# Row loads on ScalarE's queue, chunk loads first on SyncE's, GpSimd's broadcasts held back, and the first operands split by pairs

## The chip, the cores and the metric

One core of a Trainium2 chip runs the whole program. The metric is the device time of one execution in microseconds, as the median of several runs. Beside the timed runs there is one profiled execution, from which every row below is taken.

## The reference, cut to what matters

Two transformer stages run one after the other on 256 tokens of width 1024, in fp32. What matters here is how the first one begins:

```
mod   = silu(c)     @ w_ada + b_ada          # c: 1024 numbers, w_ada: 1024 x 6144
mod_c = silu(c_ctx) @ w_ada + b_ada
h  = rmsnorm(x,   g_norm1) * (1 + sc1)  + sh1
hc = rmsnorm(ctx, g_norm1) * (1 + scc1) + shc1
p, p_c = h @ w_in, hc @ w_in                 # 1024 x 2592
```

Everything after (attention, retention, the three feed-forward parts, the second stage's mixers) depends on `p` and `p_c`.

## The kernel before

**Precision by splitting.** TensorE multiplies in a fast format, so each fp32 matrix is split in two: ScalarE copies it into a rounded high part (`wh`, `hh`, `ch`), VectorE subtracts that from the original to get the low part (`wl`, `hl`, `cl`), and `three` issues three matmuls for a product (lines 1920 to 1922).

**Modulation.** The first 2048 columns of `w_ada` come as eight chunks of 128 rows, 1 MB each, `mod1_w[0]` to `mod1_w[7]`. TensorE takes them in the order 0, 1, 3, 2, 4, 5, 6, 7. Chunks 1, 2, 4, 5 and 7 are split (`mod1_high`, line 1485, on ScalarE, then `mod1_low`, line 803, on VectorE); 0, 3 and 6 are used as they are. After chunk 3 TensorE turns the small vectors, which lie as rows of `vrow`, into columns, and VectorE needs these before it normalises `ctx` and splits chunk 4. After chunk 2 TensorE turns the normalised `ctx`. After chunk 7 the sums are turned, `mod` is formed, and `mod1_ready` lets the operands be made.

**Small vectors.** `VEC_TILES` lists 16 row loads in three tiles: three with `c`, `c_ctx` and `c_2` first (`FIRST_ROWS`), eight more in tile 0, four in tile 1, one in tile 2. `in_c` counts the first three, `in_rows` the others, `in_ident` the identity matrix, a part of `con`. Before the chunks, TensorE turns the first three and ScalarE takes their silu; `cs_ready` then lets TensorE begin chunk 0.

**Queues.** SyncE issues nearly all loads, in an order written by hand: the three rows, the identity, chunks 0 to 2, the 13 remaining rows, chunk 3, `ctx`, chunks 4 and 5, `x`, chunks 6 and 7, then the units of `w_in` (each up to 1 MB, in two parts). GpSimd issues at its start four small broadcasts (`in_small`), clears `acc` and loads its bias, and loads `postg`, a 512 KB broadcast that is wanted much later. Behind these in GpSimd's program comes a wait for work of about 74 us. ScalarE issues no loads.

**The first operands.** `evac_high` (line 1462) on ScalarE and `evac_low` (line 744) on VectorE make `ch`/`cl` (N_CTX) and then `hh`/`hl` (N_X) in four pairs j of two row blocks each. For a pair, ScalarE forms block 2j in `hraw[:, 0]` and VectorE block 2j+1 in `hraw[:, 1]`, both from PSUM; then ScalarE copies both to the high part, one at a time, and VectorE subtracts, one at a time. ScalarE's second copy alone waits for VectorE's block. VectorE splits unit 1 (`take(1)`) between pairs 1 and 2 of `ctx`. TensorE starts the products of either operand when two pairs of `hraw` have been read out of PSUM (`t_raw`, `d_raw`).

Of the kernel before, what the change touches and what calls it, by code (L numbers as in the profile page):

```python
# [7 lines left out]
ALU = mybir.AluOpType  # L8
ACT = mybir.ActivationFunctionType
AX = mybir.AxisListType  # L10
F32 = mybir.dt.float32
# [4 lines left out]
P = 128  # L16
TOK = 256
# [34 lines left out]
def shape_constants():  # L52
# [19 lines left out]
    for name, f in (("cos_m", np.cos), ("sin_m", np.sin)):  # L72
# [7 lines left out]
VEC_TILES = [  # L80
# [3 lines left out]
    [("conv_w", 88 * P, 44)],  # L84
]
# [32 lines left out]
N_CTX, N_X, N_RET, N_FF0, N_MIX1, N_FF1, N_KV, N_MIX2, N_FOX, N_FF2 = range(10)  # L118
# [80 lines left out]
FIRST_ROWS = 3  # L199
# [5 lines left out]
def build(nc, a, out):  # L205

    ctx = ExitStack()
    with ctx:
# [7 lines left out]
        con = sb("con", [P, CONST_W])  # L216
# [12 lines left out]
        hraw = sb("hraw", [P, 2, HALF])  # L229
# [23 lines left out]
        vrow = junk[:, 0:3 * P].rearrange("p (t c) -> p t c", t=3)  # L253
# [127 lines left out]
        in_c = sem("in_c")  # L381
        in_ident = sem("in_ident")
# [7 lines left out]
        d_raw = sem("d_raw")  # L390
        in_rows = sem("in_rows")
# [7 lines left out]
        mod1_loaded = [sem(f"mod1_loaded{i}") for i in range(6)]  # L399
# [31 lines left out]
        t_hi = sem("t_hi")  # L431
        t_lo = sem("t_lo")
# [145 lines left out]

        taken = []

        block = ctx.enter_context(nc.Block())


        @block.vector
        def _(dve):
# [158 lines left out]
            def evac_low(n, lo, hi, pairs):  # L744

                for j in pairs:
                    k = 2 * j + 1
                    dve.wait_ge(turned, 4 * TURN_NO[n] + 2 * (j // 2) + 2)
                    dve.wait_ge(t_lo, 8 * n + max(k - 3, 0))
                    at = (j % 2) * TOK  # L750
                    nc.vector.tensor_scalar(hraw[:, 1, at:at + TOK], ps[:, TURN_BANKS[n][2 * (j // 2) + 1], at:at + TOK],  # L751
                                            mod[:, n, 0, k:k + 1], mod[:, n, 1, k:k + 1], ALU.mult, ALU.add)\
                        .then_inc(d_raw, 1)
                    for side in range(2):
                        kk = 2 * j + side
                        dve.wait_ge(t_hi, 8 * n + kk + 1)
                        nc.vector.tensor_tensor(lo[:, kk, :], hraw[:, side, at:at + TOK], hi[:, kk, :].bitcast(F32),
                                                ALU.subtract).then_inc(t_lo, 1)
# [461 lines left out]
            for t in range(NT):  # L1220
                c = R_AT[R_KH] + t * FH
# [48 lines left out]
            for t in range(NT):  # L1270
                c = R_AT[R_QH] + t * FH
# [40 lines left out]
            for h in range(FH):  # L1312
# [7 lines left out]
                else:  # L1320
                    v = FOX_ADA + h // 8
# [31 lines left out]
        def _(act):  # L1353
# [103 lines left out]
            def root_table():  # L1457

                nc.scalar.activation(credit[:, used[0]:used[0] + 1], ident[:, 0:1], ACT.Sqrt)
                used[0] += 1  # L1460

            def evac_high(n, hi, pairs):

                for j in pairs:
                    k = 2 * j
                    act.wait_ge(turned, 4 * TURN_NO[n] + 2 * (j // 2) + 1)
                    act.wait_ge(t_lo, 8 * n + max(k - 3, 0))
                    at = (j % 2) * TOK
                    nc.scalar.activation(hraw[:, 0, at:at + TOK], ps[:, TURN_BANKS[n][2 * (j // 2)], at:at + TOK],  # L1469
                                         ACT.Identity, scale=mod[:, n, 0, k:k + 1], bias=mod[:, n, 1, k:k + 1])\  # L1470
                        .then_inc(t_raw, 1)
                    act.wait_ge(t_raw, 4 * n + j + 1)
                    nc.scalar.activation(hi[:, k, :], hraw[:, 0, at:at + TOK], ACT.Copy).then_inc(t_hi, 1)
                    act.wait_ge(d_raw, 4 * n + j + 1)
                    nc.scalar.activation(hi[:, k + 1, :], hraw[:, 1, at:at + TOK], ACT.Copy).then_inc(t_hi, 1)

            def mod1_high(i, parts=(slice(0, UNIT),)):
# [6 lines left out]
                for cc in parts:  # L1484
                    nc.scalar.activation(wh[:, SPLIT_SLOT[i], cc], mod1_w[k][:, cc], ACT.Copy).then_inc(m_hi, 1)

            act.wait_ge(in_ident, 16)
            nc.scalar.activation(credit[:, 15:16], ident[:, 0:1], ACT.Silu)
            act.wait_ge(c_cols, 1)
# [3 lines left out]
                .then_inc(cs_ready, 1)  # L1493
            act.wait_ge(cs0_zero, 1)
            nc.scalar.activation(cs0[:, 0:2], cs[:, 0:16:8], ACT.Copy).then_inc(cs_ready, 1)
            root_table()
            mod1_high(0)
            mod1_high(1)
# [1108 lines left out]
        def _(pool):  # L2607
# [11 lines left out]
            def start_acc(g):  # L2619

                if g > 1:

                    pool.wait_ge(ex_done, EX_BASE[g])
                nc.gpsimd.memset(acc[:, :], 0.0).then_inc(acc_zeroed, 1)  # L2624
                pool.wait_ge(acc_zeroed, g)
                pool.dma_start(acc[0:1, :], ada[g][1]).then_inc(acc_biased, 16)
# [14 lines left out]
            def load_bc(j):  # L2641
# [5 lines left out]

            nc.gpsimd.memset(credit[:, 0:1], 0.0).then_inc(hid_pool, CREDIT)
            nc.gpsimd.memset(credit[:, 1:2], 0.0).then_inc(gl_done, CREDIT)
            pool.dma_start(lg[:, 3, :], a["ret_decay"][0].rearrange("d h -> (d h)").partition_broadcast(P))\  # L2650
                .then_inc(in_small, 16)
            pool.dma_start(bf[:, :], a["kv_b_f_2"].partition_broadcast(P)).then_inc(in_small, 16)
            pool.dma_start(gcol[0:FD, 0:1], a["b_q_norm_g_2"][0].rearrange("(d c) -> d c", c=1)).then_inc(in_small, 16)
            pool.dma_start(gcol[0:FD, 1:2], a["k_norm_g_2"].rearrange("(d c) -> d c", c=1)).then_inc(in_small, 16)
            start_acc(1)
            load_postg(0)

            pool.wait_ge(sq_done, SQ_NO[R_C, 0, 5] + 1)
# [82 lines left out]
        def _(sp):  # L2741
# [40 lines left out]
                k = v % 8  # L2782
                sp.dma_start(au[:, v % 2, :], ada[v // 8][0][k * P:(k + 1) * P, :]).then_inc(au_loaded[v % 2], 16)

            def send_rows(t, first, last):

                r = sum(n for _, _, n in VEC_TILES[t][:first])
                for name, at, n in VEC_TILES[t][first:last]:
                    v = a[name]
                    if len(v.shape) == 2:  # L2790
                        v = v.rearrange("a b -> (a b)")
                    elif len(v.shape) == 3:
                        v = v.rearrange("a b c -> (a b c)")
                    sp.dma_start(vrow[r:r + n, t, :], v[at:at + n * P].rearrange("(r c) -> r c", c=P))\
                        .then_inc(in_c if name in ("c", "c_ctx", "c_2") else in_rows, 16)
                    r += n

            def send_chunk(k):
                sp.dma_start(mod1_w[k], ada[0][0][k * P:(k + 1) * P, :])\
                    .then_inc(au_loaded[k] if k < 2 else mod1_loaded[k - 2], 16)  # L2800

            send_rows(0, 0, FIRST_ROWS)
            sp.dma_start(con[:, 0:P], a["shape_consts"][:, 0:P]).then_inc(in_ident, 16)
            for k in range(3):
                send_chunk(k)
            send_rows(0, FIRST_ROWS, len(VEC_TILES[0]))
            for t in (1, 2):
                send_rows(t, 0, len(VEC_TILES[t]))
            send_chunk(3)
            sp.dma_start(cx[:, :, :], a["ctx"][0].rearrange("(t p) d -> p t d", p=P)).then_inc(in_ctx, 16)  # L2810
            send_chunk(4)
            send_chunk(5)
# [74 lines left out]
```

## Time and profile before

| | us |
|---|---|
| median of 3 runs | 1173.5 (1172.95 to 1174.92) |
| the profiled execution, its own time | 1174.02 |
| its span from first to last instruction | 1172.2 |
| TensorE busy | 1134.3 (97%) |
| VectorE, ScalarE, GpSimd busy | 832.2, 602.7, 209.8 |

The share of TensorE is nearly full over the whole span except in the first slices, so the stretch up to about 67 us is read instruction by instruction. The 1.8 us between own time and span lie outside the instructions.

### The profile page before, as it was taken

How to read it: one execution, taken by the hardware profiler on the slowest of the kernel's cores; microseconds unless marked ns; L12 is line 12 of the kernel's file. 1: busy time of each engine (PE TensorE's matmuls, PEld its weight loads, DVE VectorE, ACT ScalarE, POOL GpSimd, SP SyncE). 2: the span in 40 equal slices, each digit the busy share in tenths (PEclk: the TensorE clock that was granted, in tenths of full speed). 3: DMA queues.
4: the chain of work that ended last, by engine and by line, in shares of the span. 5: the costliest groups of instructions: out<-in, count | busy, mean ns of one | idle time of the engine just before them, and what ended most of it. 6: DMA issues, size and time to landing. Idle time of an engine off the chain costs nothing.

```text
span 1172.2 us, 18295 instructions
## 1 busy us (share of the span) xinstructions
PE 1134.3 (97%) x7112; PEld 984.5 (84%) x7112; DVE 832.2 (71%) x908; ACT 602.7 (51%) x884; POOL 209.8 (18%) x164
## 2 busy tenths in 40 slices
PE   5899989999999999999999999999999999999998
PEld 1587747889999877798879999887878988999986
DVE  3795565778887967988777765967889797354543
ACT  4863354556665446454365444346456667444433
POOL 1037400005666302010001112100000000122200
PEclk9999999999999999999999999999999999999999
DMA  8685650148876886986547887874888334556551
GB/s 329 261 321 191 233 215 2 36 134 297 280 262 215 324 349 204 339 268 210 206 144 270 299 274 251 324 302 172 321 283 294 123 105 144 180 179 185 195 195 72
DMA packets 124304, 263.38 MB, mean 225 GB/s; under 512 B 8329, under 2 KB 76497, under 8 KB 114001
## 3 DMA queue, kind: packets, MB, share of 16 engines
q1 hardware_dynamic: 121553, 254.56, 61.6%
q0 software_dynamic: 2688, 7.95, 2.3%
q8 instruction: 43, 0.70, 0.2%
q14 instruction: 20, 0.16, 0.0%
HBM read 261.43 MB, written 1.05 MB: 224 GB/s over the span
## 4 chain that ended last, share of the span: by engine, by line
PE 79%; DVE 8%; ACT 4%; DMA 4%; issue 3%; SPq 1%; DVEq 0%; ACTq 0%
PE ps L1920 23%; PE ps L1922 23%; PE ps L1921 23%; DVE wl L599 2%; DMA raw<-in_w_in_dram 2%; PE ps L2226 1%; ACT wh L1361 1%; PE ps L2242 1%; PE ps L1961 1%; DVE vg L1155 1%; DMA raw<-in_kv_w_dram 1%; DMA raw<-in_w_down_dram 1%; PE ps L2277 1%; PE ps L2285 1%; PE ps L2234 1%
## 5 line engine op out<-in xcount | busy, mean ns | idle before, releaser
L599 DVE TENSOR_TENSOR wl<-raw,wh 128x2048 fp32r<-128x2048 f32 (+2 forms) x149 | 342.9, 2304 | 106.6 <-ACT wh L1361 105.7
L1361 ACT ACTIVATE wh<-raw 128x2048 fp32r<-128x2048 f32 (+2 forms) x148 | 278.8, 1890 | 138.2 <-DMA raw<-in_ffn_w_down_dram 52.9
L1920 PE MATMUL ps<-hh,wh 128*128 128x256 f32 (+1 forms) x1192 | 337.9, 283 | 4.7 <-DVE wl L599 3.6
L1921 PE MATMUL ps<-hl,wh 128*128 128x256 f32 (+1 forms) x1192 | 334.9, 281 | 0.0
L1922 PE MATMUL ps<-hh,wl 128*128 128x256 f32 (+1 forms) x1192 | 334.8, 281 | 0.0
L1920 PEld LDWEIGHTS ps<-hh,wh 128*128 128x128 f32 (+1 forms) x1192 | 223.9, 188 | 6.8 <-DVE wl L599 3.6
L1921 PEld LDWEIGHTS ps<-hl,wh 128*128 128x128 f32 (+1 forms) x1192 | 223.9, 188 | 0.3
L1922 PEld LDWEIGHTS ps<-hh,wl 128*128 128x128 f32 (+1 forms) x1192 | 223.8, 188 | 0.2
L1920 PE MATMUL ps<-wh,hh 128*128 128x512 f32 (+1 forms) x352 | 138.8, 394 | 5.6 <-DVE hraw L751 2.5
L611 DVE SCALAR_TENSOR_TENSOR acc<-au,cs,acc 128x2048 f32<-128x2048 f32 x53 | 129.6, 2446 | 13.2 <-DMA acc<-in_ada_b_dram 8.6
L2701 POOL TENSOR_TENSOR gl<-hid,gh 128x256 f32 (+1 forms) x66 | 78.7, 1192 | 324.8 <-ACT gh L1709 324.8
L1921 PE MATMUL ps<-wl,hh 128*128 128x512 f32 (+1 forms) x352 | 136.3, 387 | 0.0
L1922 PE MATMUL ps<-wh,hl 128*128 128x512 f32 (+1 forms) x352 | 136.3, 387 | 0.0
L1920 PE MATMUL ps<-wh,gh 128*128 128x512 f32 x264 | 104.9, 397 | 0.1
L1921 PE MATMUL ps<-wl,gh 128*128 128x512 f32 x264 | 104.3, 395 | 0.0
L1922 PE MATMUL ps<-wh,gl 128*128 128x512 f32 x264 | 104.2, 395 | 0.0
L1920 PEld LDWEIGHTS ps<-wh,hh 128*128 128x128 f32 x352 | 66.7, 190 | 23.1 <-ACT hraw L1469 2.6
L1694 ACT ACTIVATE sl<-ps 128x256 f32<-128x256 f32 x44 | 16.9, 385 | 126.4 <-PE ps L1922 126.4
L1922 PEld LDWEIGHTS ps<-wh,hl 128*128 128x128 f32 x352 | 66.7, 189 | 14.6
L1921 PEld LDWEIGHTS ps<-wl,hh 128*128 128x128 f32 x352 | 66.8, 190 | 13.6 <-issue 0.2
L2624 POOL MEMSET acc<- 128x2048 f32 x9 | 16.3, 1815 | 320.1 <-PE ps L2065 283.1
L1067 DVE TENSOR_TENSOR hid<-sl,ps 128x256 f32<-128x256 f32 x44 | 18.3, 417 | 62.1 <-ACT sl L1694 62.1
(325 smaller groups left out, 1602.1 us busy)
## 6 DMA issues: line engine op xcount, KB each, us to landing
au<-in_ada_w_dram SPq DMA_DIRECT2D x48, 1024.0 KB, 6.1
raw<-in_ffn_w_gu_dram SPq DMA_DIRECT2D x88, 512.0 KB, 4.8
raw<-in_w_up_dram SPq DMA_DIRECT2D x44, 512.0 KB, 4.8
raw<-in_ffn_w_down_dram SPq DMA_DIRECT2D x44, 512.0 KB, 4.5
au<-in_w_ada_dram SPq DMA_DIRECT2D x18, 1024.0 KB, 6.7
raw<-in_a_w_in_dram SPq DMA_DIRECT2D x32, 512.0 KB, 6.2
raw<-in_w_down_dram SPq DMA_DIRECT2D x22, 512.0 KB, 6.4
raw<-in_w_in_dram SPq DMA_DIRECT2D x16, 512.0 KB, 6.6
```

Source lines behind the costliest of these rows:

```text
L599: nc.vector.tensor_tensor(wl[:, u % RAW, 0:n], raw[:, u % RAW, 0:n], wh[:, u % RAW, 0:n].bitcast(F32), ALU.subtract).then_inc(lo_done, 1)
L611: nc.vector.scalar_tensor_tensor(acc[:, :], au[:, v % 2, :], cs[:, at:at + 1], acc[:, :], ALU.mult, ALU.add).then_inc(acc_step, 1)
L1067: nc.vector.tensor_tensor(hid[:, c, :], sl[:, c, :], ps[:, 4 + pp % 4, TOK:], ALU.mult)\
L1155: nc.vector.tensor_tensor(part, part, bcast(bc[:, j % 4, :], 1, NT), op).then_inc(affine, 1)
L1361: nc.scalar.activation(wh[:, u % RAW, 0:n], raw[:, u % RAW, 0:n], ACT.Copy).then_inc(hi_done, 1)
L1694: nc.scalar.activation(sl[:, c, :], ps[:, bank, 0:TOK], ACT.Silu).then_inc(silu_done, 1)
L1920: nc.tensor.matmul(to, lh, rh, start=start, stop=False, skip_group_check=True)
L1921: nc.tensor.matmul(to, lh, rl, start=False, stop=False, skip_group_check=True)
L1922: return nc.tensor.matmul(to, ll, rh, start=False, stop=stop, skip_group_check=True)
L1961: ins = nc.tensor.matmul(ps[:, EX_BANKS[g][0], j:j + 1], acc[:, c * P:(c + 1) * P], ones[:, 0:1], start=True, stop=True, skip_group_check= ...
L2624: nc.gpsimd.memset(acc[:, :], 0.0).then_inc(acc_zeroed, 1)
L2701: nc.gpsimd.tensor_tensor(gl[:, at_, :], hid[:, c:c + 1, :], gh[:, at_, :].bitcast(F32), ALU.subtract)\
```

## The change

Four things move. The row loads and the identity go from SyncE's program to ScalarE's: the first twelve ahead of the silu, the five of tiles 1 and 2 behind it. SyncE begins with chunks 0 to 3 and keeps the rest of its order. GpSimd clears `acc` and loads its bias first, then waits until chunk 7 has landed, and only then issues the four small broadcasts and `postg`. And for all four pairs of N_X and pairs 1 to 3 of N_CTX, ScalarE waits for both blocks and copies them in one instruction of 512 columns, and VectorE subtracts both in one.

```
+        def paired(n, j):
+            return n == N_X or (n == N_CTX and j >= 1)
...
+                    if paired(n, j):
+                        dve.wait_ge(t_hi, 8 * n + 2 * j + 2)
+                        nc.vector.tensor_tensor(lo[:, 2 * j:2 * j + 2, :], hraw[:, :, at:at + TOK],
+                                                hi[:, 2 * j:2 * j + 2, :].bitcast(F32), ALU.subtract).then_inc(t_lo, 2)
+                        continue
...
+                    if paired(n, j):
+                        act.wait_ge(d_raw, 4 * n + j + 1)
+                        nc.scalar.activation(hi[:, k:k + 2, :], hraw[:, :, at:at + TOK], ACT.Copy).then_inc(t_hi, 2)
+                        continue
...
+            send_rows(0, 0, FIRST_ROWS)
+            act.dma_start(con[:, 0:P], a["shape_consts"][:, 0:P]).then_inc(in_ident, 16)
+            send_rows(0, FIRST_ROWS, len(VEC_TILES[0]))
             act.wait_ge(in_ident, 16)
...
+            for t in (1, 2):
+                send_rows(t, 0, len(VEC_TILES[t]))
             root_table()
...
+            start_acc(1)
+            pool.wait_ge(mod1_loaded[5], 16)
             pool.dma_start(lg[:, 3, :], a["ret_decay"][0].rearrange("d h -> (d h)").partition_broadcast(P))\
                 .then_inc(in_small, 16)
...
-            start_acc(1)
             load_postg(0)
...
-            send_rows(0, 0, FIRST_ROWS)
-            sp.dma_start(con[:, 0:P], a["shape_consts"][:, 0:P]).then_inc(in_ident, 16)
-            for k in range(3):
+            for k in range(4):
                 send_chunk(k)
-            send_rows(0, FIRST_ROWS, len(VEC_TILES[0]))
-            for t in (1, 2):
-                send_rows(t, 0, len(VEC_TILES[t]))
-            send_chunk(3)
```

`send_rows` itself is moved from SyncE's program to ScalarE's, with `act.dma_start` in place of `sp.dma_start`.

## Rows read from the trace of the kernel before

**Rows 1.** Busy time from 66 us on: engines PE, PEld, DVE, ACT, POOL, clock.

```profile
66.00:1172.00 1106.00, 1085.22 (x6861) 954.96 (x6859) 793.24 (x846) 564.87 (x825) 204.31 (x151) 1.00 0.63 220
```

**Rows 2.** Stretches: us, PE, PEld, DVE, ACT, POOL busy, granted clock, DMA share, GB/s.

```profile
20.00:34.00 14.00, 12.22 (x53) 4.58 (x52) 9.78 (x15) 9.07 (x14) 0.00 (x0) 1.00 1.02 417
...
49.24:51.68 2.44, 0.00 (x0) 0.03 (x1) 1.86 (x5) 2.22 (x6) 0.00 (x0) 1.00 0.00 0
53.50:56.00 2.50, 2.50 (x13) 2.50 (x13) 1.67 (x4) 2.41 (x4) 0.00 (x0) 0.50 0.00 0
57.00:67.00 10.00, 10.00 (x80) 9.83 (x78) 8.57 (x5) 2.09 (x2) 0.00 (x0) 1.00 0.80 272
```

**Rows 3.** Timeline of ScalarE up to its first split of a chunk.

```profile
4.78 0.20 ACT L1488 ACTIVATE credit<-con 128x1 f32<-128x1 f32 x1 [2.75 <-DMA con<-in_shape_consts_dram]
...
5.69 1.28 ACT L1459 ACT_TABLE_LOAD   x1
...
13.39 1.91 ACT L1485 ACTIVATE wh<-au 128x2048 fp32r<-128x2048 f32 x1 [6.20 <-DMA au<-in_w_ada_dram]
```

**Rows 4.** Timeline of VectorE, the splits of chunks 1, 4 and 5.

```profile
15.33 2.29 DVE L803 TENSOR_TENSOR mod_l<-au,wh 128x2048 fp32r<-128x2048 f32 x1 [9.38 <-ACT wh L1485]
...
26.68 4.67 DVE L803 TENSOR_TENSOR mod_l<-mod_w,wh 128x2048 fp32r<-128x2048 f32 x2 [0.19 <-ACT wh L1485]
```

**Rows 5.** Timeline of TensorE: chunk 0, chunk 1, first product of h.

```profile
10.33 6.14 PE L2092 MATMUL ps<-au,cs 128*4 128x512 f32 x8 [5.23 <-DMA au<-in_w_ada_dram]
17.77 0.39 PE L2081 MATMUL ps<-wh,cs 128*4 128x512 f32 x1 [1.29 <-DVE mod_l L803]
...
51.68 0.35 PE L1920 MATMUL ps<-wh,hh 128*128 128x256 f32 x1 [2.45 <-DVE hraw L751]
```

**Rows 6.** Timeline of VectorE around one pair of h.

```profile
51.05 0.54 DVE L751 TENSOR_SCALAR hraw<-ps,mod 128x256 f32<-128x256 f32 x1
51.57 0.92 DVE L757 TENSOR_TENSOR hl<-hraw,hh 128x256 fp32r<-128x256 f32 x2
52.41 0.54 DVE L751 TENSOR_SCALAR hraw<-ps,mod 128x256 f32<-128x256 f32 x1
```

**Rows 7.** Timeline of SyncE's queue: start us, length us, line and operation.

```profile
0.75 0.40 SPq L2794 DMA_DIRECT2D hraw<-in_c_dram  x1
...
2.28 0.90 SPq L2799 DMA_DIRECT2D au<-in_w_ada_dram  x2
...
3.70 0.84 SPq L2794 DMA_DIRECT2D hraw<-in_g_norm_dram  x1
...
5.38 0.25 SPq L2794 DMA_DIRECT2D hraw<-in_g_ret_dram  x1
...
7.27 0.38 SPq L2794 DMA_DIRECT2D hraw<-in_conv_w_dram  x1
...
9.34 0.35 SPq L2799 DMA_DIRECT2D mod_w<-in_w_ada_dram  x1
...
14.48 18.32 SPq L2764 DMA_DIRECT2D raw<-in_w_in_dram  x8
```

**Rows 8.** Timeline of ScalarE around the same pair.

```profile
51.12 0.42 ACT L1473 ACTIVATE hh<-hraw 128x256 fp32r<-128x256 f32 x1
51.62 0.42 ACT L1475 ACTIVATE hh<-hraw 128x256 fp32r<-128x256 f32 x1
```

**Rows 9.** Instructions on the chunks' tiles: durations ns, minimum, median and maximum.

```profile
L1485 ACT ACTIVATE wh<-mod_w x5: 1042/1905/1916, 16.7 to 35.6; 128x2048 fp32r<-128x2048 f32 x3, 128x1024 fp32r<-128x1024 f32 x2
L803 DVE TENSOR_TENSOR mod_l<-mod_w,wh x5: 1220/2291/2293, 18.7 to 36.9; 128x2048 fp32r<-128x2048 f32 x3, 128x1024 fp32r<-128x1024 f32 x2
```

**Rows 10.** Timeline of ScalarE, a 512-wide instruction.

```profile
74.54 0.80 ACT L1544 ACTIVATE mask<-con,lg 128x512 f32<-128x512 f32 x1
```

**Rows 11.** Timeline of VectorE: the split of unit 5.

```profile
86.08 2.29 DVE L599 TENSOR_TENSOR wl<-raw,wh 128x2048 fp32r<-128x2048 f32 x1
```

**Rows 12.** Timeline of TensorE: the first product of unit 5.

```profile
90.39 0.39 PE L1920 MATMUL ps<-wh,hh 128*128 128x512 f32 x1
```

More of the change, by code:

```diff
@@ L1485, in mod1_high, with send_rows @@
                     nc.scalar.activation(wh[:, SPLIT_SLOT[i], cc], mod1_w[k][:, cc], ACT.Copy).then_inc(m_hi, 1)
+            def send_rows(t, first, last):
+                r = sum(n for _, _, n in VEC_TILES[t][:first])
+                for name, at, n in VEC_TILES[t][first:last]:
+                    v = a[name]
+                    if len(v.shape) == 2:
+                        v = v.rearrange("a b -> (a b)")
+                    elif len(v.shape) == 3:
+                        v = v.rearrange("a b c -> (a b c)")
+                    act.dma_start(vrow[r:r + n, t, :], v[at:at + n * P].rearrange("(r c) -> r c", c=P))\
+                        .then_inc(in_c if name in ("c", "c_ctx", "c_2") else in_rows, 16)
+                    r += n
+            send_rows(0, 0, FIRST_ROWS)
+            act.dma_start(con[:, 0:P], a["shape_consts"][:, 0:P]).then_inc(in_ident, 16)
+            send_rows(0, FIRST_ROWS, len(VEC_TILES[0]))
             act.wait_ge(in_ident, 16)
@@ L2783, in send_ada @@
                 sp.dma_start(au[:, v % 2, :], ada[v // 8][0][k * P:(k + 1) * P, :]).then_inc(au_loaded[v % 2], 16)
[L2785 to L2796, printed above, removed]
             def send_chunk(k):
```

## The prediction

> **What bounds the kernel now.** I read the shares of busy time first. From 66 us to the end TensorE is busy for 1085 of 1106 us, at its full granted clock [rows 1]. Whatever starts that stretch earlier or later therefore moves the end by as much, unless VectorE or ScalarE falls so far behind that TensorE waits. The change touches nothing after it. So I read the first 66 us, engine by engine, in the timelines.
>
> There the loads look like the limit, since they run at 417 GB/s with a full share from 20 to 34 us [rows 2], but the instruction that waits longest says otherwise from chunk 1 on. Chunk 1 lands at 13.39 us, and ScalarE, which had been idle, splits it at once [rows 3]. VectorE follows at 15.33 [rows 4], and TensorE uses it at 17.77 [rows 5]. From landing to use that is 4.38 us. From 17.77 on TensorE has almost no gap: chunk 3, the turned columns, chunk 2, the turned `ctx`, then chunk 4, which waits for VectorE. VectorE in turn had waited just 0.19 us for ScalarE at 26.68 [rows 4]; its time there comes from the turned columns, hence from TensorE. The stretch up to the operands is thus a chain through TensorE and VectorE with the loads close behind. Its start is the use of chunk 1.
>
> Then the operands are made, and TensorE waits 2.45 us for the second pair of `h` before it starts at 51.68 [rows 5]. That product has 12 matmuls to a row block; at 80 in 10 us [rows 2] these take 1.5 us, so 3.0 us to a pair, and VectorE makes a pair in 1.36 us (51.05 to 52.41, [rows 6]). After the start nothing is short; only the start counts.
>
> **The loads.** SyncE issues chunk 0 at 2.28 us and would now do so at 0.75, that is 1.53 us earlier [rows 7]. Chunk 3, now issued at 9.34, goes out before 3 us. `postg` puts 512 KB, at 417 GB/s 1.25 us of transfer, ahead of chunk 7; its issue, now among GpSimd's first, goes behind that chunk. Landings should therefore come 1.5 us earlier at the start and up to 3.5 us earlier at chunk 7. I take chunk 1 at 13.39 − 1.53 = 11.86 us at the latest.
>
> **ScalarE's queue.** Now every issue costs time on ScalarE. No row of before shows an issue there; SyncE's are the nearest. The first four took from 0.75 to 2.28, the next eight from 3.70 to 7.27, the last five from 7.27 to 9.34 [rows 7]: 1.53 + 3.57 + 2.07 = 7.17 us, 0.42 each. So the twelve end at 0.75 + 1.53 + 3.57 = 5.85. The table load of 1.28 us that now hides in the wait for the identity comes after them: 7.13. The silu and its copies take what lies between 4.78 and 5.69 [rows 3], so TensorE may begin chunk 0 at about 8.0. It takes 6.14 us [rows 5], to 14.2 us. The five others end at 10.1, the next table load and its touch (1.49) at 11.6. That is just when chunk 1 lands at the latest, so its split starts at 11.6 to 11.9 and TensorE uses it 4.38 us later, at 16.0 to 16.2 in place of 17.77. Gain 1.8 us. Two small waits go as well, VectorE's 0.19 us for chunk 4 and about as much at the second half of chunk 7: together 0.4. The head gains **2.2 us**. What is late next is again this same chain; the row loads, which `in_rows` waits for at about 22 us, are there by far.
>
> Both sides: at 0.25 us an issue (the shortest, 5.38 in [rows 7]) ScalarE is free at 8.7, chunk 0 can start at 7 and end at 13.1, and chunk 1 is used no earlier than 13.9: gain 3.9 + 0.4 = 4.3. At the other end each issue could cost more than 0.42; at 0.53 the whole gain of chunk 1 is gone, at 0.84 (3.70 in [rows 7]) it turns into a loss of 5 us. Between these I take the mean, because seventeen issues of this very kind gave it.
>
> The Trainium skill, page "DMA: Bandwidth & Descriptors", section "Issuing engines are not separate DMA queues", speaks against moving issues: the same sixteen engines carry them whoever issues, and only the issuing sequencer's time is saved. By that rule alone the head gains at most the 1.53 us of issue time ahead of chunk 0. The trace of before has one hardware queue only and can't decide it.
>
> **GpSimd's order.** The bias of `acc` comes sooner, and is first wanted when `h` is done. The four small broadcasts go out behind chunk 7, at about 31 us; ScalarE waits for them once it has made `h`, over 20 us later. Behind GpSimd's new wait stand these issues, `postg`, and then work that starts at about 74 us. Nothing is late, and the loads left then are units of `w_in`; the DMA engines are idle at 49 us (share 0.00, [rows 2]). Cost nothing; if the small ones took over 20 us, it would show as a wait before `lg`, up to what they are late.
>
> **The pairs.** Here I expect a loss. Now VectorE's step to the next pair is its own work: raw 0.52 (51.05 to 51.57), then two subtractions of 0.42 [rows 6], while ScalarE's copies run beside it: the first, at 51.12, before VectorE's block is ready, the second, at 51.62, beside the first subtraction [rows 8]. In the new form nothing overlaps: VectorE's block, then ScalarE's copy of both, then the subtraction of both. Prices: block to copy 51.62 − 51.05 = 0.57. The 512-wide copy from the slope of the 1024- and 2048-wide ones, (1.905 − 1.042)/1024 = 0.84 ns a column: 0.61, with the handover 0.65. The subtraction likewise, 1.22 − 512 × 1.046 ns = 0.68 [rows 9], of which 0.61 passes before the next may start. Sum 1.83 us for a pair against 1.36.
>
> Through the order of before: pair 0 of `ctx` is unchanged and the products of `ctx` start as now. Pair 1's subtraction delays the split of unit 1 by 0.48. Pairs 2 and 3 add 0.47 and 0.28 (one shares its time with a wait that is already there). Pair 0 of `h` adds 0.3. So the second block of `h` is ready **1.5 us** later, counted from the start of the operands, and the product of `h` with it. Bounds: if a 512-wide instruction took no longer than a 256-wide one (0.42, [rows 8]), a pair would take 0.57 + 0.46 + 0.42 = 1.45 and the delay be 0.3; with 0.80 for either, the longest 512-wide row [rows 10], a pair takes 2.1 and the delay is 2.4. I stay with the slope, which comes from the same copies and subtractions.
>
> Saved instructions elsewhere give nothing back: ScalarE and VectorE reach the later work some 1.2 us late against TensorE. The tightest place I found is the split of unit 5, which ends at 86.08 + 2.29 = 88.4 [rows 11] and is wanted at 90.39 [rows 12]. The 2.0 us of room cover it; without them it would cost the 1.2 us.
>
> **The clock.** In the 2.44 us before 51.68 TensorE does nothing, and from 53.5 to 56 its granted clock is 0.50, the 1.2 GHz level [rows 2]. At half speed for some 3 us it loses 1.5 us. The new kernel has the same idle, about 2.7 us, and a further one of 1 us within the `ctx` product. I expect the same loss again, and take 0 to 3 us in all as possible.
>
> **The sum.** Own time of the profiled execution 1174.0; head −2.2; pairs +1.5; GpSimd 0; clock 0: 1173.3 us. The median of the runs lies 0.5 under the profiled one, so I forecast **1173.0**.
>
> **Rivals.**
> (a) ScalarE's issues are cheap or the row loads free the chunks: head −4.3 us, pairs +1.5, so 1171.2, or 1170.7 as a median. For it: the table load and the issues hide before chunk 1 if they are short. Against: 0.42 us is a mean of seventeen.
> (b) The head gains only the 1.53 us of earlier issue, as the page's rule above would have it. The sum is then 1174.0 − 1.5 + 1.5 = 1174.0, or 1173.5: no change that shows.
> (c) Slower: the issues on ScalarE stall. SyncE's queue is full at 14.48, where eight issues take 18.32 us, 2.29 each [rows 7]. SyncE now fills it by about 5 us. If ScalarE's last five issues then cost 2.29, it is free 9.4 us later, at 21.0, chunk 1 is used at 25.4, and the head loses 7.6: 1174.0 + 7.6 + 1.5 = 1183. It decides once ScalarE is free later than 15.5 us. Against: the units of `w_in` that took 2.29 have many short rows, and row loads between full queues at 7 to 9 us took 0.4.
> (d) The clock is low for a second stretch, or at chunk 3: +1.5 us, 1174.5. Or not at all: 1171.5.
> (e) The pairing does not lengthen the path, because VectorE's wait overlaps something not seen: 1171.5.
>
> **How the numbers follow.** The forecast with its neighbour (b), 1172 to 1174.5: 0.45. Case (a) 0.15, (e) and no low clock 0.15, (d) slower 0.13, (c) in some degree 0.12. Within 0.2% is 2.35 us, about what a measurement can tell here: 1171.15 to 1175.85. Case (a) is faster by that in full, (e) and no low clock in most of their cases, the forecast in some where its terms are all at the good end: faster 0.36. Slower are (c) and a part of (d): 0.17. Same 0.47. The range 1170.0 to 1176.5 leaves out (c) and the far end of (a). The forecast's own range is 1171.5 to 1174.7.
>
> **What would show it.** ScalarE's queue: seventeen issues, the silu after 7 us, free near 11.6. Chunk 1 used at about 16 us; chunk 7 landed near 31 and the operands begun near 39.4, not 41.55. Pairs of `h` at 1.83 us on VectorE, with a wait for ScalarE in each; the product of `h` near 51.0. A pace of 1.4 us there would prove the pair term wrong; a ScalarE busy with issues past 13 us, or chunk 1 used before 15, the head term.

## The result, and the profile after

The changed kernel takes 1177.44 us (1175.38 to 1179.29) against 1173.96 (1172.95 to 1175.84) for the kernel before, 20 runs of each on one chip. The ratio is 1.0026, with a 95% interval of 1.0020 to 1.0032: **3.1 us slower** (the medians lie 3.5 apart; every difference below is taken from the ratio). In the tests below a few executions ran far longer than the rest, up to 2877 us, and count in the medians but not in the ratios. The forecast was 1173.0 and the range ended at 1176.5; the prediction had given slower a chance of 0.17, and for another reason.

The profiled execution took 1178.46 us with a span of 1176.6, 4.4 more than before. I read the rows in the order of the prediction's steps. First ScalarE's timeline (start us, duration, line, operation; in brackets the idle time before it and what ended it):

```profile
0.74 0.60 ACTq L1509 DMA_DIRECT2D hraw<-in_c_dram  x1
...
2.03 0.41 ACTq L1514 DMA_DIRECT2D con<-in_shape_consts_dram  x1
...
5.77 1.28 ACT L1517 ACT_TABLE_LOAD   x1 [5.77 <-issue]
9.96 0.20 ACT L1517 ACTIVATE credit<-con 128x1 f32<-128x1 f32 x1 [2.92 <-DMA con<-in_shape_consts_dram]
...
12.41 1.28 ACT L1468 ACT_TABLE_LOAD   x1 [1.55 <-issue]
...
13.81 1.89 ACT L1498 ACTIVATE wh<-au 128x2048 fp32r<-128x2048 f32 x1
...
40.90 0.56 ACT L1478 ACTIVATE hraw<-ps,mod 128x256 f32<-128x256 f32 x1
```

The issues are as priced: twelve between 0.74 and 5.74 us, 0.42 each, and five from 10.55 to 12.37, 0.36 each. But the silu, which was to run as soon as they and the table load were over (7.05), waits 2.92 us more for the identity, and starts at 9.96. The same 64 KB landed by 4.78 in [rows 3]. The row of the issues (queue, size, us from issue to landing) says how long it was under way:

```profile
con<-in_shape_consts_dram ACTq DMA_DIRECT2D x1, 64.0 KB, 7.9
```

So the five other issues and the second table load, which are behind the silu, end at 13.69, and chunk 1 is split at 13.81. This row has no wait in brackets: the chunk lay there already. In [rows 3] ScalarE had stood ready for 6.20 us instead. TensorE's timeline shows the rest of the head:

```profile
9.99 0.30 PE L2102 MATMUL ps<-con,hraw 24*128 24x24 f32 x1 [9.99 <-DMA con<-in_shape_consts_dram]
10.91 5.27 PE L2123 MATMUL ps<-au,cs 128*4 128x512 f32 x8 [0.63 <-ACT cs L1524]
18.18 0.39 PE L2112 MATMUL ps<-wh,cs 128*4 128x512 f32 x1 [2.00 <-DVE mod_l L812]
...
53.22 0.36 PE L1951 MATMUL ps<-wh,hh 128*128 128x256 f32 x1 [2.83 <-DVE hraw L755]
```

Chunk 0 starts at 10.91 (before 10.33), chunk 1 is used at 18.18 (before 17.77, [rows 5]), 0.41 later. From there to the operands TensorE and VectorE need 22.72 us instead of 23.78, since the small waits on the way are gone: 1.06 less, where 0.4 had been priced. So the operands begin at 40.90, 0.65 earlier than the 41.55 of before, where 2.2 had been promised. The product of `h` starts at 53.22, 1.54 later than in [rows 5]. From the start of the operands to it are 12.32 us instead of 10.13, so the pairs cost 2.19. VectorE's timeline has one pair of `h`:

```profile
52.58 0.54 DVE L755 TENSOR_SCALAR hraw<-ps,mod 128x256 f32<-128x256 f32 x1
53.97 0.69 DVE L760 TENSOR_TENSOR hl<-hraw,hh 128x512 fp32r<-128x512 f32 x1 [0.85 <-ACT hh L1484]
54.58 0.54 DVE L755 TENSOR_SCALAR hraw<-ps,mod 128x256 f32<-128x256 f32 x1
```

A pair is now 54.58 − 52.58 = 2.00 us against the 1.36 of [rows 6]. VectorE idles 0.85 of it for ScalarE.

The stretches (columns as in [rows 2]) show the loads from 5 to 10 us, the clock around the product of `h`, and the long rest:

```profile
5.00:10.00 5.00, 0.01 (x1) 0.01 (x1) 0.00 (x0) 1.32 (x2) 0.00 (x0) 1.00 1.02 417
...
53.20:56.40 3.20, 3.18 (x25) 3.20 (x26) 1.58 (x3) 2.17 (x4) 0.00 (x0) 1.00 0.01 3
66.00:1176.00 1110.00, 1086.31 (x6861) 955.00 (x6859) 796.03 (x848) 565.52 (x825) 200.88 (x151) 1.00 0.63 221
```

From 5 us on the DMA engines are already full (1.02), so the identity travels in a crowd. From 53.20 to 56.40 the granted clock is 1.00, its 2.4 GHz level. That gives back the 1.5 us that the profile before lost at 0.50 [rows 2], and at 67.91 us TensorE is where it was before (67.90). The rest takes 1110 us instead of the 1106 of [rows 1], with only 1.1 us more of TensorE's work in it, so TensorE must wait. It does so at the first product of each unit:

```profile
67.91 0.50 PE L1951 MATMUL ps<-wh,hh 128*128 128x512 f32 x1 [0.84 <-ACT kpe L1555]
...
79.90 0.50 PE L1951 MATMUL ps<-wh,hh 128*128 128x512 f32 x1 [0.55 <-DVE wl L603]
...
91.71 0.47 PE L1951 MATMUL ps<-wh,hh 128*128 128x512 f32 x1 [0.34 <-DVE wl L603]
...
103.80 0.47 PE L1951 MATMUL ps<-wh,hh 128*128 128x512 f32 x1 [0.65 <-DVE acc L615]
```

Unit 4's product starts at 79.90, unit 5's at 91.71 and the next at 103.80. Before, they started at 79.19, 90.39 [rows 12] and 101.59. TensorE loses 0.7, then 0.6, then 0.9, together 2.2 us. The waits for VectorE in brackets make 1.5 of it. VectorE's and GpSimd's timelines show what it was doing:

```profile
76.45 3.39 DVE L603 TENSOR_TENSOR wl<-raw,wh 128x2048 fp32r<-128x2048 f32 x1
...
89.27 2.29 DVE L603 TENSOR_TENSOR wl<-raw,wh 128x2048 fp32r<-128x2048 f32 x1
```

```profile
76.15 1.54 POOL L2699 TENSOR_TENSOR mask<-mask,gate 128x512 f32<-128x512 f32 x1 [0.68 <-ACT gate L1577]
78.08 2.90 POOL L2699 TENSOR_TENSOR mask<-mask,gate 128x512 f32<-128x512 f32 x1 [0.39 <-ACT gate L1577]
```

VectorE has finished `h` at 58.66, before at 55.2, so the split of unit 4 starts at 76.45 in place of 73.74. There GpSimd adds masks at the same time, and the split takes 3.39 us instead of 2.29. The one of unit 5, with nothing beside it, takes 2.29 but starts 3.2 us later than in [rows 11].

In the profile before, VectorE's split was the first to start, at 73.74, and GpSimd was the one to be held up. Its copy of a 128x128 tile began beside that split and took 2.00 us; after the change, with VectorE on other work, the same copy took 0.47:

```profile
74.18 2.00 POOL L2660 CAST ident_r<-con 128x128 fp32r<-128x128 f32 x1 [67.40 <-ACT hraw L1378]
```

```profile
74.20 0.47 POOL L2693 CAST ident_r<-con 128x128 fp32r<-128x128 f32 x1 [41.12 <-ACT hraw L1387]
```

Adding up: head −0.65, pairs +2.19, clock −1.5, waits at units 4 to 6 +2.2. That makes 2.2 of the profile's 4.4 us. The other 2.2 arise in a few small steps between 300 and 540 us. The section on why the prediction was wrong takes them up.

### The profile page after: what moved, and what is told of

The parts are those of the page before. It is cut to its first block, busy times and chain, and to the rows that moved or that the text cites. A ratio compares the mean times of both kernels' runs of the same rounds, so it can differ in the third digit from the quotient of the medians.

```text
span 1176.6 us, 18295 instructions
## 1 busy us (share of the span) xinstructions
PE 1132.8 (96%) x7112; PEld 982.8 (84%) x7112; DVE 831.0 (71%) x901; ACT 601.8 (51%) x877; POOL 206.9 (18%) x164
## 4 chain that ended last, share of the span: by engine, by line
PE 77%; DVE 10%; issue 5%; ACT 4%; DMA 3%; ACTq 0%; DVEq 0%; SPq 0%
PE ps L1951 22%; PE ps L1953 22%; PE ps L1952 22%; DVE acc L615 2%; DVE wl L603 2%; PE ps L2257 1%; PE ps L2273 1%; PE ps L1992 1%; DMA au<-in_w_ada_dram 1%; DMA raw<-in_kv_w_dram 1%; ACT wh L1370 1%; DMA con<-in_shape_consts_dram 1%; DMA bc<-in_a_ln_b_dram 1%; DVE acc L719 1%; PE ps L2308 1%
## 5 line engine op out<-in xcount | busy, mean ns | idle before, releaser
L2731 POOL TENSOR_TENSOR hid<-sl,hu 128x256 f32<-128x256 f32 x22 | 55.1, 2505 | 44.3 <-ACT sl L1731 44.3
```

The lines of the kernel that those rows point to most:

```text
L2731: nc.gpsimd.tensor_tensor(hid[:, c, :], sl[:, c, :], hu[:, c, 0, :], ALU.mult).then_inc(hid_pool, 1)
```

## The experiments

Each kernel was timed beside the kernel before, in turn with it.

**The loads alone.** The changed kernel without pairing:

```
         def paired(n, j):
-            return n == N_X or (n == N_CTX and j >= 1)
+            return False
```

> The changed kernel without the pairing: loads reordered and GpSimd held as in the change, first operands split one block at a time. Theory P (the pairing costs the time: it lengthens the making of the operands by 2.2 us and leaves VectorE 3 us late, so that TensorE waits for units 4 and 5 and for acc): operands begin near 40.9 us, the product of h near 51.0, unit 4 starts with no wait for VectorE's split, and the time is 0 to 1.5 us under the kernel before (1172.5 to 1174). Theory L (the late identity and the row loads on ScalarE's queue cost it): 1176 to 1178, the same as the changed kernel.

Measured: 1174.64 us, ratio 1.0003 (0.9994 to 1.0012). ScalarE's timeline of this kernel repeats the one above:

```profile
9.92 0.20 ACT L1517 ACTIVATE credit<-con 128x1 f32<-128x1 f32 x1 [3.04 <-DMA con<-in_shape_consts_dram]
...
40.83 0.56 ACT L1478 ACTIVATE hraw<-ps,mod 128x256 f32<-128x256 f32 x1
```

The product of `h` starts at 50.95, as expected, but the time is 0.4 us above before and not 0 to 1.5 under it. The loads as a whole gain nothing that shows. That the late identity is what eats their gain is tested below.

**The pairs alone.** The kernel before with `paired` and its three uses added, as in the diff.

> The kernel before with the pairing alone. Theory P: the product of h starts 2.2 us later than before (near 53.9), a pair of h takes 2.00 us, unit 4's split ends after TensorE wants it, and the time is 3 to 4 us above the kernel before (1177 to 1178). Theory L: no change, 1174.

Measured: 1177.36 us, 1.0028 (1.0016 to 1.0040), +3.3 us. The head is the one of before, and ScalarE waits for chunk 1 to land:

```profile
13.36 1.91 ACT L1498 ACTIVATE wh<-au 128x2048 fp32r<-128x2048 f32 x1 [6.24 <-DMA au<-in_w_ada_dram]
```

The product of `h` starts at 53.86, 2.18 later. The whole loss is in the pairs, and twice the 1.5 us that I had priced. The part of the expectation on unit 4 did not come: its split started before GpSimd's additions did, and TensorE did not wait for it. The split of this kernel:

```profile
77.23 2.38 DVE L603 TENSOR_TENSOR wl<-raw,wh 128x2048 fp32r<-128x2048 f32 x1
```

It takes 2.38 us and not 3.39, and TensorE loses only 0.7 us between the start of the product and the first product after unit 5, 0.5 of it waiting for `acc`. The clock tells the two profiles apart: in this one it is low behind the start of the product, as before, so TensorE reaches these units 1.5 us later. The section on why the prediction was wrong comes back to this.

**GpSimd's hold alone**, which I had put at nothing:

```
+            start_acc(1)
+            pool.wait_ge(mod1_loaded[5], 16)
             pool.dma_start(lg[:, 3, :], a["ret_decay"][0]...
...
-            start_acc(1)
             load_postg(0)
```

> The kernel before with GpSimd's five broadcasts held until the last chunk, and nothing else. Theory P: chunk 7 lands about 1 us earlier, which nobody waits for; the use of chunk 1 may come some tenths earlier; time within 1 us of the kernel before. Theory H (the held broadcasts fall among the units of w_in and come late where they are wanted): a wait before lg or for unit 1, 1175 to 1177.

Measured: 1171.36 us, 0.9973 (0.9963 to 0.9984), **3.2 us faster**. ScalarE's timeline:

```profile
3.69 0.20 ACT L1488 ACTIVATE credit<-con 128x1 f32<-128x1 f32 x1 [1.66 <-DMA con<-in_shape_consts_dram]
...
9.90 1.91 ACT L1485 ACTIVATE wh<-au 128x2048 fp32r<-128x2048 f32 x1 [3.81 <-DMA au<-in_w_ada_dram]
...
38.35 0.56 ACT L1469 ACTIVATE hraw<-ps,mod 128x256 f32<-128x256 f32 x1
```

The identity is there at 3.69 instead of 4.78, chunk 1 at 9.90 instead of 13.39, and the operands begin 3.2 us earlier. Neither expectation had allowed for that: the time was to stay within 1 us, or to rise. The stretch from 5 to 10 us, first before, then with the hold (the last three columns are clock, DMA share, GB/s):

```profile
5.00:10.00 5.00, 0.10 (x1) 0.00 (x0) 0.18 (x1) 1.99 (x5) 1.49 (x3) 1.00 0.88 333
```

```profile
5.00:10.00 5.00, 2.49 (x3) 0.37 (x4) 0.00 (x0) 1.17 (x3) 0.00 (x0) 1.00 1.01 426
```

The engines were 0.88 busy before and moved 333 GB/s; with GpSimd's broadcasts held they move 426. That is 0.47 MB more in these 5 us, almost half a chunk.

**Which broadcasts?** Hold only the four small ones (`load_postg(0)` stays ahead of the wait), or hold only `postg`:

```
             start_acc(1)
+            load_postg(0)
             pool.wait_ge(mod1_loaded[5], 16)
             pool.dma_start(lg[:, 3, :], ...          # the four small ones
-            load_postg(0)
```

> The kernel before with the four small broadcasts of GpSimd held until the last chunk, and the 512 KB one (postg) still issued at the start. Theory S (many tiny packets from GpSimd's queue hold up the first chunk): chunk 1's split begins near 10, nearly all of the 3.1 us that holding all five gave, about 1171.5 to 1172. Theory B (the bytes of postg do it, 1.25 us of transfer): chunk 1's split begins at 12 to 13, 1173 to 1174.

> The kernel before with only postg held until the last chunk, and the four small broadcasts still at the start. Theory S: chunk 1's split begins within 1 us of 13.4, 1173.3 to 1174.3. Theory B: near 10 to 11, 1171 to 1172.

Measured: small ones held 1172.46 us, 0.9982 (0.9973 to 0.9991), −2.1; `postg` held 1173.02, 0.9990 (0.9981 to 0.9999), −1.2. Chunk 1's split in the one and in the other:

```profile
10.82 1.91 ACT L1485 ACTIVATE wh<-au 128x2048 fp32r<-128x2048 f32 x1 [4.71 <-DMA au<-in_w_ada_dram]
```

```profile
12.69 1.91 ACT L1485 ACTIVATE wh<-au 128x2048 fp32r<-128x2048 f32 x1 [5.53 <-DMA au<-in_w_ada_dram]
```

The two add up to 3.3, the whole gain of the hold. Chunk 0 starts at 7.58 with the small ones held and at 10.26 with `postg` held (10.33 before): some 12 KB of small broadcasts delay the first megabyte by 2.7 us. The 512 KB of `postg` cost about the 1.2 us that they take at 417 GB/s; the interval reaches from 0.1 to 2.2. So neither theory holds alone: the small ones gave two thirds and not nearly all, `postg` the rest.

Two things stay open here. Holding the small ones also lets GpSimd issue `acc`'s bias at 2.92 instead of 5.73 and `postg` at 3.56 instead of 6.23, so that run moves more than its name says (against what it gained, if anything, since more then travels early). And no run tells whether it is the number of their packets, their issues or their place ahead of chunk 0 that makes so few bytes so dear.

**The identity first.** The loads of the changed kernel, unpaired, but `c`, `c_ctx`, `c_2` and the identity are SyncE's again, ahead of chunk 0; ScalarE keeps the 13 other rows:

```
-            send_rows(0, 0, FIRST_ROWS)
-            act.dma_start(con[:, 0:P], a["shape_consts"][:, 0:P]).then_inc(in_ident, 16)
             send_rows(0, FIRST_ROWS, len(VEC_TILES[0]))
...
+            for r, name in enumerate(("c", "c_ctx", "c_2")):
+                v = a[name].rearrange("a b -> (a b)") if len(a[name].shape) == 2 else a[name]
+                sp.dma_start(vrow[8 * r:8 * r + 8, 0, :], v.rearrange("(r c) -> r c", c=P)).then_inc(in_c, 16)
+            sp.dma_start(con[:, 0:P], a["shape_consts"][:, 0:P]).then_inc(in_ident, 16)
             for k in range(4):
```

> As the loads-only kernel (no pairing), but the three first rows and the identity are issued by SyncE ahead of chunk 0; ScalarE issues only the other thirteen rows. Theory P with the reading that the head gained only 0.6 us because the identity landed at 9.9 us behind the chunks: the identity lands before 6 us, the silu runs near 6.5, chunk 1 is used at 16 to 16.5 us, the operands begin near 39.5 to 40, and the time is 1171 to 1172.5. If the identity's landing is not what holds the head, it is as the loads-only kernel, within 0.5 us.

Measured: 1170.44 us, 0.9969 (0.9958 to 0.9979), **−3.6 us**, and as 1170.60, 0.9961, when run again. It beats both kernels, and the expected 1171 to 1172.5. Most of this is the hold, which gave 3.2 alone; the 0.4 between them is within the intervals, so no run shows that having ScalarE issue the 13 rows gains anything of its own. ScalarE's timeline:

```profile
5.11 0.20 ACT L1515 ACTIVATE credit<-con 128x1 f32<-128x1 f32 x1
...
8.69 0.20 ACT L1468 ACTIVATE credit<-con 128x1 f32<-128x1 f32 x1
10.18 1.91 ACT L1498 ACTIVATE wh<-au 128x2048 fp32r<-128x2048 f32 x1 [1.28 <-DMA au<-in_w_ada_dram]
...
37.62 0.56 ACT L1478 ACTIVATE hraw<-ps,mod 128x256 f32<-128x256 f32 x1
```

The issues now hide before chunk 1, which lands at 10.18 with ScalarE idle for 1.28 us.

**The identity as ScalarE's own first issue**, so that only its place in ScalarE's order differs:

```
-            send_rows(0, 0, FIRST_ROWS)
             act.dma_start(con[:, 0:P], a["shape_consts"][:, 0:P]).then_inc(in_ident, 16)
-            send_rows(0, FIRST_ROWS, len(VEC_TILES[0]))
+            send_rows(0, 0, len(VEC_TILES[0]))
```

> As the loads-only kernel, but ScalarE issues the identity as its first load, at 0.75 us in place of 2.03, ahead of the rows. If the identity is late because chunks already stand on the same sixteen engines when it comes, it lands at 4 to 6 us, not at 9.9, chunk 1's split begins near 10.5 to 11.5 (after ScalarE's issues), and the time is 1.5 to 3 us under the loads-only kernel. If a load on ScalarE's queue is slow beside SyncE's chunks whatever its place, it still lands 7 to 8 us after its issue and the time is that of the loads-only kernel.

Measured: 1171.96 us, 0.9976 (0.9967 to 0.9985), −2.8. Its issue row:

```profile
con<-in_shape_consts_dram ACTq DMA_DIRECT2D x1, 64.0 KB, 5.3
```

It is issued at 0.74 instead of 2.03 and is then under way for 5.3 us instead of 7.9. Chunk 1 is used at 15.79 instead of the 18.13 of the loads alone, and the 3 us are back, as expected. The place of the identity's issue among ScalarE's, against SyncE's chunks, is the cause, and not the number of issues on ScalarE, which is the same.

**Chunk 3 ahead of the 13 rows**, with the hold, all on SyncE (`for k in range(4)`, the later `send_chunk(3)` dropped).

> All loads on SyncE's queue, GpSimd's broadcasts held, no pairing; the only other edit is that chunk 3 is issued before the thirteen rows. Since chunk 3 is not what TensorE waits for once chunk 1 is used at 14.3, at most 0.5 us under the kernel with the hold alone: 1170.8 to 1171.6. If chunk 3 or what follows it in the queue still holds the head, 1 us or more under it.

Measured: 1171.68 us, 0.9971 (0.9960 to 0.9983). The same as the hold alone: an earlier chunk 3 is worth nothing, since chunk 1 sets the pace.

**Parts of the pairing.** Only pairs 2 and 3 of `h`, which come behind the start of its product: `return n == N_X and j >= 2`. And the subtraction of both blocks at once for all seven pairs, with ScalarE's two copies left apart (the diff's part in `evac_low` alone).

> The kernel before with pairing for pairs 2 and 3 of h alone, which are made after the product of h has started. Theory G (the pairing costs because it puts off the start of that product, and nothing else): the product starts near 51.7, VectorE ends the operands 1.2 us later but within the room of units 3 to 5, time as before, within 0.7 us. Theory V (what costs is VectorE's lateness at units 4, 5 and acc): TensorE waits for units 4 or 5, 0.5 to 1.5 us above before.

> The kernel before with the subtraction of a pair in one instruction, but ScalarE's two copies apart as before, in the same seven pairs. If the cost of the pairing is the lost overlap between the engines, half of it comes back: a pair of h takes 0.57 + 0.45 + 0.65 = 1.67 us in place of 2.00 (and of 1.36 before), the product of h starts about 1.1 us after before's, and the time is 1.0 to 2.0 us above before (1175.3 to 1176.3). If the cost is in the 512-wide copy or subtraction itself (rows 0.5 us apart in the output), it stays near 3 or goes to 0.

Measured: late pairs 1175.16 us, 1.0008 (0.9998 to 1.0017); one subtraction 1175.75, 1.0010 (1.0001 to 1.0019). VectorE's timeline in the second:

```profile
52.38 0.54 DVE L755 TENSOR_SCALAR hraw<-ps,mod 128x256 f32<-128x256 f32 x1
53.47 0.69 DVE L760 TENSOR_TENSOR hl<-hraw,hh 128x512 fp32r<-128x512 f32 x1 [0.56 <-ACT hh L1484]
54.08 0.54 DVE L755 TENSOR_SCALAR hraw<-ps,mod 128x256 f32<-128x256 f32 x1
```

The pair is 1.70 us and the product of `h` starts at 53.02, +1.34. So the overlap of copies and subtractions is lost in two halves: 0.34 us by waiting for both copies, 0.30 more by making one copy of them. Late pairs alone leave the start at 51.69 and cost nothing that shows (0.9, with an interval from −0.2 to 2.0).

**Pairing on top of the best kernel**, all seven pairs, then only pairs 2 and 3 of `h`:

> The identity-first kernel with the pairing added in all seven pairs. If the loads and the pairing add up, 3.1 us above the identity-first kernel: about 1173.5, the same as the kernel before. If VectorE's lateness was only harmful with the late head, less: 1171.5 to 1172.5.

> The identity-first kernel with pairing for pairs 2 and 3 of h alone. In the profile of the identity-first kernel TensorE's clock does not fall in the product of h, so it reaches units 4 to 6 earlier against VectorE than in the kernel before, and room is smaller. Theory G (only the start of the product of h counts): no change against the identity-first kernel, 1170.4 beside a kernel before at 1174.4, ratio 0.9969. Theory V (VectorE's lateness costs as well where the clock stays up): TensorE waits for the split of unit 4 or 5 or for acc, 0.5 to 2 us in all, ratio 0.9975 to 0.9985.

Measured: all pairs 1173.93 us, 0.9993 (0.9984 to 1.0002), that is 0.0024 or 2.8 us above the best kernel; late pairs 1171.16, 0.9969 (0.9956 to 0.9981), the same as the best kernel. TensorE's waits from 62 to 110 us (us in all, count, longest) with all pairs, and with the late ones:

```profile
PE ps L1949 <- DVE wl L603: 0.9, 2, 0.5
PE ps L1949 <- ACT kpe L1553: 0.8, 1, 0.8
PE ps L1949 <- DVE acc L615: 0.7, 1, 0.7
```

```profile
PE ps L1949 <- ACT kpe L1553: 0.8, 1, 0.8
PE ps L1949 <- DVE acc L615: 0.7, 1, 0.7
```

With all pairs two of the waits are for the splits of units 4 and 5, 0.9 us together. With the late ones these are gone, but the 0.7 for `acc` stays, where the best kernel has 0.2; so late pairs are not quite free in a profile, even though the timed runs show no cost. The split of unit 4 takes 3.38 us beside GpSimd in the first, as in the changed kernel.

**The clock.** The best kernel was run a second time.

> The identity-first kernel once more, beside the run with late pairs on the same chip, so that the two can be set against each other: ratio to the kernel before 0.9969 again, within 0.0010.

In both of its profiles TensorE has been idle for 2.48 us when the product of `h` starts (47.74 and 47.99). The stretch from 49 to 50 us, in the first and in the second:

```profile
49.00:50.00 1.00, 1.00 (x10) 1.00 (x10) 0.94 (x4) 0.93 (x3) 0.00 (x0) 1.00 0.03 8
```

```profile
49.00:50.00 1.00, 1.00 (x6) 1.00 (x6) 0.94 (x3) 0.96 (x3) 0.00 (x0) 0.50 0.02 8
```

2.4 GHz in the one, 0.50 and so 1.2 GHz in the other, which reaches the same matmul at 57.04 us in place of 55.34. Whether the dip comes is a matter of the execution, not of the kernel, at least here. Of the 15 profiles of this case 8 have it, all behind an idle time of TensorE of 2.45 to 2.83 us, and the 7 without it had the same idle time.

## Why the prediction was wrong

Two steps failed. The first is **ScalarE's queue**: it let the silu run at about 8.0 us, as soon as the issues and the table load were over, and so took over the identity's landing from before. The identity landed at 9.9 us, and the loads that were to gain 2.2 us measured +0.4 by themselves. The second is **the path of the pairs** with its "2.0 us of room": priced at 1.5 us, it measured +3.3 by itself. These are misses of 2.6 and 1.8 us, 4.4 together with intervals of about 1 us each, against a forecast that was 3.6 us too low relative to the kernel before.

The table compares, in the profile of each kernel, where TensorE starts the product of `h` and where it starts the first product after unit 5 (51.68 and 101.59 us before), with what the runs measured (ratio less one, times 1174). "Low clock" says whether TensorE's granted clock was 0.50 behind the start of the product, as in the profile before.

| kernel | product of `h`, us later | low clock | after unit 5, us later | measured, us |
|---|---|---|---|---|
| small broadcasts held | −1.8 | no | −3.1 | −2.1 |
| `postg` held | −1.3 | no | −2.4 | −1.2 |
| both held | −3.2 | yes | −3.2 | −3.2 |
| loads, changed kernel | −0.7 | no | −1.8 | +0.4 |
| loads, identity ScalarE's first | −3.1 | yes | −3.0 | −2.8 |
| loads, identity first on SyncE | −3.9 | no | −5.1 | −3.6 |
| the last with all pairs | −1.8 | no | −1.2 | −0.8 |
| late pairs alone | 0.0 | yes | 0.0 | +0.9 |
| one subtraction | +1.3 | yes | +1.6 | +1.2 |
| pairs alone | +2.2 | yes | +2.8 | +3.3 |
| changed kernel | +1.5 | no | +2.2 | +3.1 |

"Only the start counts" held in all kernels without pairing to 0.3 us, the loads alone excepted (1.1, its interval being ±1.0). The three kernels with all pairs lie 1.0 to 1.6 above it. The parts add up: loads +0.4 and pairs +3.3, 3.7 against +3.1 together, within their intervals.

The columns "low clock" and "after unit 5" show where the 1.0 to 1.6 come from. Without pairing, a profile without the low clock gains 1.1 to 1.3 us between the two places, and one with it gains nothing. With all pairs it is +0.7 in either case: when the clock stays up, TensorE comes 1.5 us earlier to units 4 to 6 and waits there for a VectorE that is late. So the pairing costs 0.7 us more than the later start in one sort of execution and, against an unpaired kernel, 1.9 in the other. With the clock low in 8 of 15 profiles an average of about 1.3 us would follow, an estimate that fits the measured 1.0 to 1.6; the timed runs do not separate the two sorts.

- **"GpSimd's order … Cost nothing."** Wrong, by 3.2 us, with the sign of a gain. I looked only for what would be late behind the new wait, and not for what the removed issues had held up. The rows of the window 5 to 10 us, with a share of 0.88 and 333 GB/s beside the 417 of [rows 2], would have shown it.
- **ScalarE's queue.** The price of 0.42 us an issue and the order on ScalarE were right; the silu "at about 8.0" was not. I had carried over the landing of the identity, 2.75 us of wait in [rows 3], to a kernel in which four chunks are issued on another queue beside it. It took 7.9 us. With the identity first the product starts 3.9 us earlier, and in the changed kernel's loads 0.7: this step cost 3.2 us, ate all that the hold gave, and left 0.65 of the promised 2.2. The start of chunk 0 was read wrongly besides: in [rows 5] it waits for its own load until 10.33, so 1.53 us earlier would be 8.8, not 8.0. It would end at 14.9, still ahead of the 16.0 of chunk 1, so the forecast did not hang on it; the bound with chunk 0 at 7 and a gain of 4.3 did. I had made a rival of issues that stall, (c), but none of a load that does. Nor was it (b), whose number, 1173.5, the loads alone come near by chance.
- **The page's rule.** The head did not gain 1.53 us by earlier issue either. The Trainium skill, page "DMA: Bandwidth & Descriptors", section "Issuing engines are not separate DMA queues", says that all loads run on the same sixteen engines and interleave, and that another issuing engine saves only issue time. The runs agree: ScalarE's queue was no way round SyncE's chunks, since the identity took 7.9 us against the 2.9 of before, and the 13 rows on ScalarE gained 0.4 us over the hold alone, within the intervals. The latency is the part that mattered.
- **The pairs, +1.5.** Right in mechanism and sign, mis-sized: 2.19. A pair took 2.00 and not 1.83 us, since both handovers are longer than priced: block to copy 0.65 and copy to subtraction 0.74, for 0.57 and 0.65; subtraction to next block 0.61 was right. The 0.17 too little counts at each of the four pairs on the path, pairs 1 to 3 of `ctx` and pair 0 of `h`, and makes the 0.7.
- **"The 2.0 us of room cover it."** Wrong. VectorE leaves `h` some 3 us later, not 1.2, and units 4 and 5 and `acc` come late. I had looked for the tightest place with the durations of before, at the places of before, and with the low clock of before: 1.5 us of the room was TensorE's own slowness. The changed kernel's profile has 2.2 us of waits there, the pairs alone 0.7. The long split of unit 4 (3.39 us) is not needed for it, since in the pairs alone it took 2.38. The delay of pairs 2 and 3 of `h` alone is not enough for it: the late pairs cost nothing that shows.
- **The clock, 0 (0 to 3).** The profile shows −1.5, and the repeated kernel shows that this is chance. It was also not a term of its own: here the waits at units 4 to 6 took it back. The single profiles differ by it, which is why the timed ratios decide.
- **The sum** was rounded up: 1173.3 less 0.5 is 1172.8, not 1173.0.

**Open.** The last 2.2 us of the profile, between 300 and 540 us. The kernels issue the same 7112 matmuls in the same order, so each can be set against its twin before. From 250 to 560 us TensorE falls 2.1 us further behind in the changed kernel, but also 2.2 and 1.5 in the two profiles of the best kernel and 1.8 with the identity as ScalarE's first, which have no pairing, and only 0.4 with the pairs alone. So they do not need the pairs, and in one and the same kernel they are 1.5 us once and 2.2 the other time. The first of the steps are waits of TensorE for VectorE's splits: from 300 to 345 us one of 0.5 us before, four with 1.2 us together in the changed kernel, four with 1.0 in the second profile of the best one. Why those splits come later in some executions no run tells, nor why the loads alone came out 1.1 us above the rule of the table.

That VectorE and GpSimd hold each other up at unit 4 is read from who started first. In the changed kernel GpSimd's addition ran from 76.15 to 77.69, the split started inside it at 76.45, and it took 1.10 us longer than alone; 1.24 were left of the addition. GpSimd's next addition started inside the split, at 78.08, and took 2.90 us instead of 1.54. Before, the copy that started inside the split ended at 76.18, 0.15 us after it. The Trainium skill, page "SBUF — State Buffer", section "SBUF: two separate sides", says that a VectorE instruction with two operands in SBUF and a GpSimd instruction that reads SBUF need the same pair of ports, and that the first to start keeps it for its whole length. The trace agrees in both directions, by the numbers just given. No run moved GpSimd's additions away.

## What to carry to other kernels

When loads are moved, follow the one that the first instruction waits for, however small: here it had to be issued ahead of the large loads, whichever queue it was on. Ask of removed or postponed transfers what they had held up, and read the DMA rate of the first microseconds against the steady one. Merging two instructions of a chain that runs between engines costs the overlap of their halves; behind the start of the product, off that chain, it cost nothing that shows and gained nothing either. And room that is read from one profile holds only for the clock of that profile.

## What the runs showed of the hardware

- Four small broadcasts of GpSimd (4, 8, 0.2 and 0.2 KB) at the start delayed the first 1 MB chunk by 2.7 us and the identity by 1.1; holding them was worth 2.1 us of the whole.
- A load of 64 KB landed 7.9 us after its issue on ScalarE's queue beside SyncE's chunks, 5.3 us when it was ScalarE's first, and 2.9 us after it when SyncE issued it ahead of the chunks, 1.8 with GpSimd's broadcasts held back.
- An issue on ScalarE took 0.36 to 0.42 us on average, the first one 0.60, and the table load stood behind them until 5.77 us.
- A split of 2048 columns on VectorE took 3.39 us when it started inside one of GpSimd's additions and 2.29 without; a copy of GpSimd's took 2.00 us when it started inside such a split and 0.47 without.
- After 2.45 to 2.83 us of idle time TensorE's granted clock fell to 0.50 (1.2 GHz) in 8 of 15 profiles and stayed at 1.00 in 7, in both ways with one and the same kernel. The low stretch was worth 1.5 us.
